# Two transformer blocks on one core: ten of twelve modulation parts summed on VectorE from transposed weight tiles, gates by way of DRAM, weights and vectors packed by the host

## The chip, the cores and the metric

The kernel runs on one core of a Trainium2 chip. The metric is the device time of one execution in microseconds (us), lower is better. Everything is float32 in and out.

## What is computed

Two transformer blocks are applied to 256 latent tokens of width 1024, beside 256 context tokens. Block 1 has two layers, whose normed inputs are scaled and shifted, and whose outputs are gated, by a *modulation* of a conditioning vector:

```
mod  = silu(c)     @ ada_w[l] + ada_b[l]         # latent: six vectors of 1024 per layer
modc = silu(c_ctx) @ ada_w[l][:, :n] + ada_b[l]  # context: six in layer 0, two in layer 1
a    = rms_norm(h, g) * (1 + sc1) + sh1;  h = h + g1 * mixer(a)
a    = rms_norm(h, g) * (1 + sc2) + sh2;  h = h + g2 * ffn(a)
```

Layer 0 mixes by a gated convolution and a neighbourhood attention (8 heads, latent and context tokens) and has a dense FFN (hidden width 2816). Layer 1 mixes by a windowed attention (8 heads) and a differential attention (4 heads), for the latent tokens alone, and has a mixture of 8 experts, two per token. Block 2 (a dilated and a latent attention, an MLP of 4096) has no modulation. The modulation is 12 *parts* of 1024 columns of `ada_w`, 4 MB each: 48 MB of weights for a product with one or two vectors.

## The kernel before

**Products.** Every float32 matmul is three products of rounded parts: ACT writes `hi`, a rounded copy of a weight tile (line 1184), VectorE writes `lo`, the rest (line 1704), and TensorE makes low by high, high by low and high by high (`mm3`, lines 722 to 724).

**Weight tiles.** All weights pass as tiles of up to 128 x 2048 floats (1 MB) in one list, in the order in which TensorE uses them, through *slots* of SBUF: three that are always there, four more in the start, one more (`slot_f`) in the FFN. The SP queue issues the loads in list order; each waits until the slot's tile before has been consumed (lines 2669, 2670). ACT and VectorE run their programs strictly in order. Before they wait for a product of TensorE, they call `feed(event)`, which makes the hi or lo of every tile that stands less than `ahead` places behind the tiles used at that event (`next_tiles`, line 486). `ahead` is 4 in the start and 2 after it.

**Modulation.** `MODS` (line 409) lists the 12 parts. Each half of 512 columns takes two tiles. `mod_product` (lines 767 to 781) makes 8 matmuls of 4 x 512 outputs per tile; VectorE copies the row out of PSUM (line 1762); POOL loads the bias beside it by a DMA (line 2553); `mod_spread` turns the row into a column per vector (line 797) or, for the gates (parts 2, 5, 10, 11), spreads it over 128 partitions (line 791); VectorE (line 1772) or ACT (line 1226 on) copies that out. Parts 0 and 1 (shift and scale of layer 0) come first of all. The rest are *filler*, written by a generator that yields between other steps: parts 2, 3, 4 in the steps of layer 0's attention `a0`, five fillings per part spread over its first 15 of 39 steps; parts 5 to 9 in the FFN, a tile after each of the w1 and w3 tiles; parts 10 and 11 in the first 10 steps of layer 1's attention `a1`. The line numbers of the generators: 800 (TensorE), 1238 (ACT), 1775 (VectorE), 2555 (POOL).

**Order of work.** Start (parts 0 and 1, norm) to 64 us; layer 0 projections (75 to 205: q, v, k, then the convolution's c, u, g twice, 12 tiles; VectorE norms the heads of q and k, lines 1794 to 1798, with a power on POOL, line 2569, in the middle, and scales and splits the turned heads, lines 1989 and 1709); POOL adds masks to the position biases (line 2600); `a0` (210 to 358); output product and norm; FFN (434 to 850); norm; layer 1 projections (884 to 985, 9 tiles, `odd_unit`, line 2125); `a1` from 1000; mixture of experts (1247 to 1572, with its tail to 1640); block 2 to the end. In an attention VectorE takes the row maxima of a unit (head and token tile, line 1903), ACT the exponentials, TensorE the transposes and the product with v, three (`a0`) or two (`a1`) steps later.

**Start.** ACT's queue issues the constants, some 18 small vectors (line 1316) and the four token tiles; TensorE turns the vectors into columns `VT`; ACT takes their silu (line 1322).

```
        def next_tiles(at, *events):
            ...
            if t.gate != at["gate"] or t.slot not in at["slots"] or i >= n + at["ahead"] or (t.prev is not None and t.prev > n - 2):
                return
```

## Time and profile before

| | |
|---|---|
| median of three runs | 2158.98 us (2157.37 to 2165.85) |
| the profiled execution's own time | 2171.43 us |
| its span on the core | 2169.6 us |
| granted TensorE clock, mean | 0.89 of full speed |
| busy: PE / VectorE / ACT / POOL | 88% / 56% / 41% / 6% |
| read from HBM | 325.8 MB, mean 151 GB/s |

Times in a row are microseconds from the start of the span unless ns is said. PE is TensorE's matmuls, PEld its weight loads, DVE is VectorE, SP the queue that loads the weights. The clock is a share of 2.4 GHz: 1.00 or 0.50 (1.2 GHz) at any moment, a mean in between over a stretch.

### The profile page before, as it was taken

What the parts mean: (1) busy time and instruction counts of PE and PEld (TensorE: products, weight loads), DVE (VectorE), ACT (ScalarE), POOL (GpSimd) and SP (SyncE); (2) the same over time, 40 slices, a digit from 0 to 9 for tenths busy, and PEclk for the clock granted to TensorE, in tenths of its full rate; (3) what the DMA queues carried; (4) which work ended last, traced back from release to release, by engine and by line L of the source; (5) the groups of instructions that cost most, each with busy time, mean ns of one, the idle gap of its engine ahead of it and who ended that gap; (6) DMA issues with size and microseconds to landing.
All of it is one profiled execution on the core that took longest, in us unless ns stands there. A gap on an engine that the chain in (4) does not pass through costs nothing. (4 is left out here: it accounts for less than half of the span.)

```text
span 2169.6 us, 22152 instructions
## 1 busy us (share of the span) xinstructions
PE 1915.4 (88%) x9060; PEld 1545.3 (71%) x9060; DVE 1206.3 (56%) x1520; ACT 898.3 (41%) x1044; POOL 125.7 (6%) x128
## 2 busy tenths in 40 slices
PE   5899899699999997795876999999995999796997
PEld 2777468577787775582655888888885966676986
DVE  5465443344433442545563888888885545456643
ACT  5323432343313331423332676767763442334542
POOL 1130000200020002112001000000000000000000
PEclk9999776889999998796677899999998995797999
DMA  6433330234434442223204699999973640125653
GB/s 243 117 97 117 98 97 12 86 117 136 150 107 140 137 150 79 83 78 97 78 1 140 221 328 329 324 325 325 326 263 128 197 141 0 59 78 165 185 188 113
DMA packets 190860, 328.44 MB, mean 151 GB/s; under 512 B 17358, under 2 KB 90512, under 8 KB 190751
## 3 DMA queue, kind: packets, MB, share of 16 engines
q1 hardware_dynamic: 185712, 321.54, 44.0%
q10 hardware_dynamic: 4208, 5.27, 0.8%
q8 instruction: 75, 1.23, 0.2%
q0 software_dynamic: 832, 0.13, 0.0%
q14 instruction: 33, 0.27, 0.0%
HBM read 325.81 MB, written 1.11 MB: 151 GB/s over the span
## 5 line engine op out<-in xcount | busy, mean ns | idle before, releaser
L1704 DVE TENSOR_TENSOR wlo__60<-raw__59,whi__61 128x2048 fp32r<-128x2048 f32 (+3 forms) x73 | 163.1, 2235 | 136.9 <-ACT whi__61 L1184 136.8
L1704 DVE TENSOR_TENSOR wlo__63<-raw__62,whi__64 128x2048 fp32r<-128x2048 f32 (+3 forms) x73 | 151.2, 2072 | 122.7 <-ACT whi__64 L1184 122.7
L1704 DVE TENSOR_TENSOR wlo__66<-raw__65,whi__67 128x2048 fp32r<-128x2048 f32 (+3 forms) x72 | 156.1, 2168 | 105.0 <-ACT whi__67 L1184 104.9
L1184 ACT ACTIVATE whi__61<-raw__59 128x2048 fp32r<-128x2048 f32 (+3 forms) x73 | 133.1, 1824 | 125.8 <-DMA raw__59<-in_ffn_w 39.3
L1184 ACT ACTIVATE whi__64<-raw__62 128x2048 fp32r<-128x2048 f32 (+3 forms) x73 | 123.7, 1694 | 137.3 <-DMA raw__62<-in_ada_w 38.2
L1184 ACT ACTIVATE whi__67<-raw__65 128x2048 fp32r<-128x2048 f32 (+3 forms) x72 | 130.7, 1815 | 97.0 <-DMA raw__65<-in_ada_w 25.4
L2569 POOL TENSOR_TENSOR keep__55<-keep__55,keep__56 128x1 f32<-128x1 f32 (+3 forms) x48 | 45.4, 946 | 1219.9 <-DVE keep__55 L1714 1219.9
L1903 DVE TENSOR_REDUCE keep__55<-ps 128x1 f32<-128x256 f32 (+1 forms) x104 | 56.6, 544 | 46.4 <-PE ps L724 39.6
L1704 DVE TENSOR_TENSOR wlo__210<-raw__209,whi__211 128x2048 fp32r<-128x2048 f32 x24 | 54.8, 2285 | 4.0 <-ACT whi__211 L1184 4.0
L1704 DVE TENSOR_TENSOR wlo__213<-raw__212,whi__214 128x2048 fp32r<-128x2048 f32 x24 | 54.8, 2284 | 0.0
L1704 DVE TENSOR_TENSOR wlo__216<-raw__215,whi__217 128x2048 fp32r<-128x2048 f32 (+1 forms) x24 | 50.6, 2109 | 3.8 <-ACT whi__217 L1184 3.8
L1704 DVE TENSOR_TENSOR wlo__133<-raw__132,whi__134 128x2048 fp32r<-128x2048 f32 (+2 forms) x14 | 28.9, 2064 | 40.5 <-ACT whi__134 L1184 40.5
L722 PE MATMUL ps<-ffn__113,wlo__133 128*128 128x512 f32 x112 | 45.1, 403 | 7.0 <-DVE wlo__133 L1704 7.0
L1184 ACT ACTIVATE whi__211<-raw__209 128x2048 fp32r<-128x2048 f32 x24 | 45.8, 1907 | 7.1 <-DMA raw__209<-in_moe_w 7.1
L1184 ACT ACTIVATE whi__214<-raw__212 128x2048 fp32r<-128x2048 f32 x24 | 45.9, 1911 | 6.3 <-DMA raw__212<-in_moe_w 6.1
L723 PE MATMUL ps<-ffn__114,whi__134 128*128 128x512 f32 x112 | 44.6, 399 | 0.0
L724 PE MATMUL ps<-ffn__113,whi__134 128*128 128x512 f32 x112 | 44.6, 398 | 0.0
L1184 ACT ACTIVATE whi__217<-raw__215 128x2048 fp32r<-128x2048 f32 (+1 forms) x24 | 42.6, 1773 | 3.4 <-DMA raw__215<-in_moe_w 2.9
L1184 ACT ACTIVATE whi__134<-raw__132 128x2048 fp32r<-128x2048 f32 (+2 forms) x14 | 24.2, 1727 | 44.5 <-DMA raw__132<-in_ffn_w 34.5
L722 PE MATMUL ps<-ffn__113,wlo__66 128*128 128x512 f32 x96 | 37.6, 392 | 0.0
L724 PE MATMUL ps<-ffn__113,whi__67 128*128 128x512 f32 x96 | 37.4, 390 | 0.0
L723 PE MATMUL ps<-ffn__114,whi__67 128*128 128x512 f32 x96 | 37.4, 389 | 0.0
(1082 smaller groups left out, 5645.4 us busy)
## 6 DMA issues: line engine op xcount, KB each, us to landing
raw__209<-in_moe_w SPq DMA_DIRECT2D x24, 1024.0 KB, 6.4
raw__212<-in_moe_w SPq DMA_DIRECT2D x24, 1024.0 KB, 6.9
raw__215<-in_moe_w SPq DMA_DIRECT2D x16, 1024.0 KB, 5.9
raw__65<-in_moe_w SPq DMA_DIRECT2D x16, 1024.0 KB, 6.2
raw__59<-in_moe_w SPq DMA_DIRECT2D x16, 1024.0 KB, 7.1
raw__65<-in_ada_w SPq DMA_DIRECT2D x14, 1024.0 KB, 5.2
raw__59<-in_ada_w SPq DMA_DIRECT2D x13, 1024.0 KB, 5.2
raw__62<-in_ada_w SPq DMA_DIRECT2D x13, 1024.0 KB, 5.2
```

Of the source, the lines that this page charges most:

```text
L722: e.matmul(out, ll, rh, start=start, stop=False)
L723: e.matmul(out, lh, rl, start=False, stop=False)
L724: return e.matmul(out, lh, rh, start=False, stop=stop)
L1184: e.activation(t.hi(), t.raw(), ACT.Copy).then_inc(*did("hi", i))
L1704: e.tensor_tensor(t.lo(), t.raw(), t.hi().bitcast(F32), ALU.subtract).then_inc(*did("lo", i))
L1903: e.tensor_reduce(neg, b[:, 0:u.total], AX.X, ALU.max).then_inc(*link())
L2569: e.tensor_tensor(x, x, EXPO[:, 0:1].broadcast_to([128, n_]) if n_ > 1 else EXPO[:, 0:1], ALU.pow).then_inc(*did(out, *key))
```

## The change

- **Sums.** Parts 2 to 11 are no longer products. The host transposes their columns of `ada_w`; a tile holds two blocks of 128 columns, a column per partition and its 1024 weights along the partition. VectorE multiplies a block with the row silu(c) or silu(c_ctx), which lies in all 128 partitions (`CB`), and adds up in the same instruction: two (parts 8 to 11) or four (parts 2 to 7) instructions of 1024 elements per tile, each waiting for the one before; then a small addition of the bias per part. ACT skips these tiles and TensorE has nothing to do with them, except for the gates.
- **Places.** A sum tile stands in the list behind each weight tile, one by one: 12 (parts 2, 3, 4) from the first tile of layer 0's projections, 20 (5 to 9) from the first of the FFN (into the w2 tiles), 8 (10, 11) from the first of layer 1's projections. `next_tiles` counts them as tiles, with `ahead` as before. The filler in `a0`, FFN and `a1` is gone.
- **Gates.** The sums of a gate are turned by TensorE, copied by VectorE, written to DRAM by POOL's queue and read back as a row into 128 partitions by a second DMA that waits for the first: parts 2 ahead of `a0`, 5 behind the first half of w1 and w3, 10 and 11 one behind the other ahead of `a1`.
- **Start.** One DMA brings all vectors, already turned. Two DMAs of 512 KB bring the broadcast rows c and c_ctx on ACT's queue behind the token tiles; ACT waits for them and takes silu of 128 x 2048 before its first `hi`. The start has five more slots, not four.
- **Packing.** Every weight tile lies in DRAM as 128 rows of up to 8 KB, one per partition; before a row was 1, 1.5, 2 or 4 KB of the weight matrix.
- Some buffers are placed anew; ACT no longer waits for the bias scratch (`rp2`), POOL does.

The core of the diff:

```diff
+    def of(self, arrays):
+        x = arrays[self.name][tuple(slice(*p) if isinstance(p, tuple) else p for p in self.at)]
+        x = x.T if self.turned else x
+        k, n = x.shape[0] // 128, x.shape[1]
+        return x.reshape(k, 128, n).transpose(1, 0, 2).reshape(-1)
...
-    slot_e = [slot(WORK + n) for n in (0, 4096)] + [slot(WORK + n) for n in (10240, 14336)]
+    slot_e = [slot(WORK + n) for n in (0, 4096, 14336, 18432, 22528)]
```

TensorE: a sum tile behind each consumed tile, and the gates.

```diff
+        def sums(p, jj):
+
+            l, part = MODS[p][:2]
+            o = part * D + jj * 256
+            i = state["tile"]
+            state["tile"] += 1
+            if book.counting:
+                src = W["ada_w"][l, :, o:o + 256].t()
+                packed.place(src)
+                s = min(open_slots, key=lambda s: last_in.get(s, s - 100))
+                TILES.append(Tile(src, 2, 1024, s, last_in.get(s), ""))
+                TILES[i].sums, TILES[i].done = (p, jj), ("msum", p, jj)
+                last_in[s] = i
+
+        def gate_rows(p):
+            n = 8 * MODS[p][3]
+            b = take("6", "gt", p)
+            for s, n_ in state["due"](("gsum", p)):
+                e.wait_ge(s, n_)
+            tr(b[0:n, 0:128], GM_OF[p][:, 0:n]).then_inc(*done("gt", p))
+
         def consumed(t, *event):
             t.done = event
+            for p, jj in itertools.islice(state["sums"], 1):
+                sums(p, jj)
 
...
         rdy = lambda N: (lambda t, k: normed(N, t // 2))
-        w_ev = I["ev_w_in"][0]
+        w_ev = W["ev_w_in"][0]
+        state["sums"] = iter([(p, jj) for p in (2, 3, 4) for jj in range(4)])
         proj(("l0", "q"), x4(AT4a), 4, KT, w_ev[:, 1536:2048], 512, rdy("a"))
...
-        fill = modulation([5, 6, 7, 8, 9], "7")
+        state["sums"] = iter([(p, jj) for p in (5, 6, 7, 8, 9) for jj in range(4)])
         nf = normed("f", 0) + normed("f", 1)
         for blk in range(2):
             bs = slice(blk * 1408, (blk + 1) * 1408)
             for f0 in range(0, 11, 2):
                 m = min(2, 11 - f0)
-                feat(("ff1", blk, f0), AT4f, I["ffn_w1"][0][:, bs], f0, m, 512, nf, "7")
```

ACT: the start, and the tiles that it passes over.

```diff
+                if t.sums:
+                    continue
                 for s, n in due((f"raw{t.slot}", i)):
                     e.wait_ge(s, n)
                 e.activation(t.hi(), t.raw(), ACT.Copy).then_inc(*did("hi", i))
...
-        for s, n in due(("z_vr",)):
-            e.wait_ge(s, n)
-        for i, (o, src) in enumerate(vec_loads):
-            e.dma_start(o, src).then_inc(*did("vec", *([i] if i + 1 < len(vec_loads) else []), by=16))
+        e.dma_start(VT[:, 0:sum(n for _, n in VECTORS)], I["vectors"]).then_inc(*did("vt", by=16))
         for t in range(4):
             e.dma_start(h_t[t], xs_d[t]).then_inc(*did("d_x", *([t] if t < 3 else []), by=16))
-        feed(("vt_t",))
+        for v, x in enumerate((I["c"], I["c_ctx"].rearrange("(o n) -> o n", o=1))):
+            e.dma_start(CB[:, v * D:(v + 1) * D], x.broadcast_to([128, D])).then_inc(
+                *did("d_cb", *([] if v else [v]), by=16))
         for s, n in due(("vt",)):
             e.wait_ge(s, n)
         e.activation(SM[:, 24:40], VT[:, 0:16], ACT.Silu).then_inc(*did("silu"))
         high("stq_hi", (), STQ[:, :, 0:2], SM[:, 24:40].rearrange("p (v k) -> p k v", v=2), ("silu",))
+        for s, n in due(("d_cb",)):
+            e.wait_ge(s, n)
+        e.activation(CB, CB, ACT.Silu).then_inc(*did("cb"))
```

VectorE: the sums and the gates' copy.

```diff
+                    summed(i, t)
+                    continue
                 for s, n in due(("hi", i)):
                     e.wait_ge(s, n)
                 e.tensor_tensor(t.lo(), t.raw(), t.hi().bitcast(F32), ALU.subtract).then_inc(*did("lo", i))
+
+        def summed(i, t):
+            p, jj = t.sums
+            gate, nv = MODS[p][3], vectors_of(p)
+            for s, n in due((f"raw{t.slot}", i), ("cb",), *gm_free(p)):
+                e.wait_ge(s, n)
+            for c in range(2):
+                for v in range(nv):
+                    k = 2 * jj + c
+                    x = GM_OF[p][:, v * 8 + k:v * 8 + k + 1] if gate else MODT_OF[p][:, 2 * k + v:2 * k + v + 1]
+                    junk = slot_sum[t.slot][:, (c * nv + v) % 2 * 1024:(c * nv + v) % 2 * 1024 + 1024]
+                    m = e.scalar_tensor_tensor(out=junk, in0=slot_raw[t.slot][:, c * 1024:c * 1024 + 1024], scalar=1.0,
+                                               in1=CB[:, v * D:(v + 1) * D], op0=ALU.mult, op1=ALU.mult, accum_out=x)
+                    if (c, v) == (1, nv - 1):
+                        m.then_inc(*did("msum", p, jj))
+                    elif v == nv - 1:
+                        m.then_inc(*link())
+                        for s, n in linked():
+                            e.wait_ge(s, n)
+            if jj < 3:
+                return
+            l, part = MODS[p][:2]
+            bias = VT[:, VROW["ada_b"] + l * 48 + part * 8:VROW["ada_b"] + l * 48 + part * 8 + 8]
+            for s, n in due(("msum", p, 3)):
+                e.wait_ge(s, n)
+            if gate:
+                x, b3 = v3(GM_OF[p][:, 0:8 * nv], nv), bias.rearrange("p (o k) -> p o k", o=1).broadcast_to([128, nv, 8])
+            else:
+                x = MODT_OF[p].rearrange("p (k v) -> p k v", v=2)[:, :, 0:nv]
+                b3 = bias.rearrange("p (k o) -> p k o", o=1).broadcast_to([128, 8, nv])
+            e.tensor_tensor(x, x, b3, ALU.add).then_inc(*did("gsum" if gate else "spr", p))
+
+        def gate_rows(p):
+            n_ = 8 * MODS[p][3]
+            feed(("gt", p))
+            for s, n in due(("gt", p), *([("gw", past_gate(p))] if past_gate(p) else [])):
+                e.wait_ge(s, n)
+            e.tensor_copy(G16[0:n_, :], bank("gt", p)[0:n_, 0:128]).then_inc(*did("gcp", p))
+            empties(("gt", p), ("gcp", p))
 
         def low(name, key, dst, src, hi, *events):
```

POOL: the gates by way of DRAM. SP: the packed loads.

```diff
+        def gate_rows(p):
+            n_ = MODS[p][3]
+            rows = scr_d["gates"][p, 0:n_ * D]
+            for s, n in due(("gcp", p)):
+                e.wait_ge(s, n)
+            e.dma_start(rows.rearrange("(r c) -> r c", c=128), G16[0:8 * n_, :]).then_inc(*did("gw", p, by=16))
+            for s, n in due(("gw", p), *row_free(p)):
+                e.wait_ge(s, n)
+            e.dma_start(MODS[p][2], rows.rearrange("(o n) -> o n", o=1).broadcast_to([128, n_ * D])).then_inc(
+                *did("sprb", p, by=16))
...
+                w_ = t.k * t.n
+                src = bass.AP(tensor=I[t.src.name].tensor, offset=packed.place(t.src), ap=[[w_, 128], [1, w_]])
+                e.dma_start(slot_raw[t.slot][:, 0:w_], src).then_inc(*did(f"raw{t.slot}", i, by=16))
```

## Rows read from the trace of the kernel before

**Rows 1.** Page: busy time of each engine; chain that ended last, by engine
```profile
PE 1915.4 (88%) x9060; PEld 1545.3 (71%) x9060; DVE 1206.3 (56%) x1520; ACT 898.3 (41%) x1044; POOL 125.7 (6%) x128
...
PE 19%; DVE 2%; ACT 1%; issue 1%; DMA 1%; POOL 0%; ACTq 0%; POOLq 0%; DVEq 0%
```

**Rows 2.** Stretches of time: length, busy us of each engine, clock, DMA
```profile
75.00:205.00 130.00, 126.40 (x567) 104.27 (x566) 70.34 (x73) 36.97 (x37) 25.41 (x12) 0.99 0.31 99
...
312.00:362.00 50.00, 48.49 (x200) 42.12 (x200) 17.21 (x49) 14.06 (x45) 0.00 (x0) 0.50 0.00 1
...
488.00:814.00 326.00, 325.73 (x1447) 252.64 (x1446) 136.73 (x110) 103.03 (x86) 17.12 (x15) 1.00 0.42 137
...
1062.00:1100.00 38.00, 38.00 (x160) 32.24 (x159) 19.05 (x46) 12.28 (x30) 0.00 (x0) 0.50 0.00 0
...
1247.00:1572.00 325.00, 322.13 (x1618) 273.81 (x1617) 285.60 (x221) 228.64 (x201) 0.00 (x0) 1.00 0.93 326
```

**Rows 3.** Stretch 434 to 868, three answers: PE's lines 778, 797, 791 alone
```profile
434.00:868.00 434.00, 40.35 (x160) 13.54 (x160) 0.97 0.39 127
...
434.00:868.00 434.00, 8.39 (x64) 7.70 (x64) 0.97 0.39 127
...
434.00:868.00 434.00, 3.96 (x8) 1.32 (x8) 0.97 0.39 127
```

**Rows 4.** Durations (ns, min/median/max) of two VectorE forms: lines 2355 and 2030
```profile
L2355 DVE TENSOR_TENSOR moe__188<-moe__188,keep__54 x1: 1225/1225/1225, 1636.6 to 1636.6; 128x1024 f32<-128x1024 f32 x1
...
L2030 DVE SCALAR_TENSOR_TENSOR in__82<-in__85,keep__51,in__82 x1: 753/753/753, 172.0 to 172.0; 128x512 f32<-128x512 f32 x1
```

**Rows 5.** Start: median landing of the last ACT loads, then ACT's first and eighth hi
```profile
keep__50<-in_ctx ACTq DMA_DIRECT2D x2, 512.0 KB, 10.6
...
10.90 1.91 ACT L1184 ACTIVATE whi__61<-raw__59 128x2048 fp32r<-128x2048 f32 x1
...
31.48 1.92 ACT L1184 ACTIVATE whi__61<-raw__59 128x2048 fp32r<-128x2048 f32 x1 [0.67 <-DMA raw__59<-in_ada_w]
```

**Rows 6.** Timeline of VectorE, layer 0 projections: start, duration, what it waited for
```profile
86.56 2.29 DVE L1704 TENSOR_TENSOR wlo__63<-raw__62,whi__64 128x2048 fp32r<-128x2048 f32 x1 [1.62 <-ACT whi__64 L1184]
...
101.16 0.69 DVE L1798 TENSOR_TENSOR in__80<-ps,keep__55 128x512 f32<-128x512 f32 x1 [1.75 <-POOL keep__55 L2569]
...
143.00 6.12 DVE L1704 TENSOR_TENSOR wlo__60<-raw__59,whi__61 128x2048 fp32r<-128x2048 f32 x1
```

**Rows 7.** Timeline of POOL, layer 0 projections
```profile
142.32 4.65 POOL L2600 TENSOR_TENSOR in__75<-in__75,keep__49 128x2048 f32<-128x2048 f32 x1
```

**Rows 8.** Timeline of VectorE, first attention: row maxima, one per unit
```profile
209.82 0.69 DVE L1903 TENSOR_REDUCE keep__55<-ps 128x1 f32<-128x512 f32 x1
...
312.78 0.42 DVE L1903 TENSOR_REDUCE keep__55<-ps 128x1 f32<-128x256 f32 x1 [1.81 <-PE ps L724]
...
316.36 0.42 DVE L1903 TENSOR_REDUCE keep__55<-ps 128x1 f32<-128x256 f32 x1 [2.97 <-PE ps L724]
...
339.02 0.42 DVE L1903 TENSOR_REDUCE keep__55<-ps 128x1 f32<-128x256 f32 x1 [1.69 <-PE ps L724]
...
341.32 0.42 DVE L1903 TENSOR_REDUCE keep__55<-ps 128x1 f32<-128x256 f32 x1 [1.26 <-PE ps L724]
```

**Rows 9.** Timeline of VectorE, layer 1 projections: first evacuation
```profile
901.84 0.68 DVE L1794 TENSOR_REDUCE keep__55<-odd__171 128x8 f32<-128x512 f32 x1
...
913.33 0.69 DVE L2143 TENSOR_TENSOR odd__166<-odd__166,odd__170 128x512 f32<-128x512 f32 x1 [1.37 <-POOL odd__170 L2632]
```

**Rows 10.** Timeline of VectorE, window attention: row maxima, one per unit
```profile
1002.48 0.69 DVE L1903 TENSOR_REDUCE keep__55<-ps 128x1 f32<-128x512 f32 x1
...
1061.36 0.69 DVE L1903 TENSOR_REDUCE keep__55<-ps 128x1 f32<-128x512 f32 x1
...
1087.16 0.69 DVE L1903 TENSOR_REDUCE keep__55<-ps 128x1 f32<-128x512 f32 x1
```

**Rows 11.** DMA issues in 985 to 1065: bias load by POOL, KB, us to landing
```profile
keep__57<-in_ada_b POOLq DMA_DIRECT2D x2, 2.0 KB, 2.7
```

More of the change, by code:

```diff
@@ L486, in next_tiles @@
     def next_tiles(at, *events):
-        n = max(place[event] for event in events)
+        n = max([place[event] for event in events], default=0)
         while at["tile"] < len(TILES):
@@ L681, in tensor_program @@
         due = Due(book)
-        state = dict(tile=0, due=due, gate="")
+        state = dict(tile=0, due=due, gate="", sums=iter(()))
         open_slots, turn_of = [0, 1, 2] + slot_e, Counter()
@@ L827, in attend @@
             A = HEADS[st]
-            fill = modulation(A.fill, "5")
-            per = -(-5 * len(A.fill) // len(A.units))
             for i in A.steps():
@@ L878, in attend @@
                     m.then_inc(*done("fin", st, g))
-                for _ in range(per):
-                    next(fill, None)
-            for _ in fill:
-                pass
         def head_turn(key, src, n, ready, ring="8"):
@@ L1258, in attend @@
             A = HEADS[st]
-            fill = modulation(A.fill)
-            per = -(-5 * len(A.fill) // len(A.units))
             for i in A.steps():
@@ L1403, in scalar_program @@
                     feed(("prod", "ff2", blk, half, t))
-        for _ in fill:
-            pass
         over = [("prod", "ff2", 1, 1, 3)]
@@ L1884, in attend @@
             A = HEADS[st]
-            fill = modulation(A.fill)
-            per = -(-5 * len(A.fill) // len(A.units))
             for i in A.steps():
@@ L1945, in attend @@
                     empties(("fin", st, g), ("flo", st, g))
-                for _ in range(per):
-                    next(fill, None)
-            for _ in fill:
-                pass
         def gated(stage, half, t, bk, g, tmp, *events):
@@ L2601, in gpsimd_program @@
                             ALU.add).then_inc(*did("bm", t))
-        for _ in modulation(HEADS["a0"].fill):
-            pass
+        gate_rows(2)
         for half in range(2):
@@ L2608, in gpsimd_program @@
             norm_rsqrt("f", t)
-        fill = modulation([5, 6, 7, 8, 9])
         for blk in range(2):
-            for _ in range(12):
-                next(fill, None)
+            if blk == 0:
+                gate_rows(5)
             for half in range(2):
@@ L2615, in gpsimd_program @@
                     residual(("ff2", blk), half, t, TMPf[t])
-        for _ in fill:
-            pass
         for t in range(4):
@@ L2633, in gpsimd_program @@
                 m.then_inc(*did("orp", kind, t))
-        for _ in modulation(HEADS["a1"].fill):
-            pass
+        gate_rows(10)
+        gate_rows(11)
         for g in (2, 3):
```

325 lines of the change are left out of this document (150 added, 175 removed).

## The prediction

> **What bounds the kernel now.** I read the page first. TensorE is busy 88% of the span, and in the chain that ended last it has 19%, DMA 1% [rows 1]. So the end is TensorE's program plus the stretches in which TensorE waits for somebody. Then I read the stages, since the share is an average of unlike ones [rows 2]. In the FFN (488 to 814) TensorE is busy all of 326 us at full clock, and VectorE 42% of it: what is taken from TensorE there comes off the time. In the expert stage TensorE has 322 of 325 us while DMA is at 0.93 of its share: TensorE bounds, narrowly. In the layer 0 projections it has 126 of 130 us, at 0.99. In the tail of `a0` (312 to 362), without filler, TensorE looks busy (48 of 50 us) but at 0.50, which is 1.2 GHz, with small matmuls; the same in `a1` behind its filler (1062 to 1100). There the steps set the pace, and the clock sets the steps.
>
> **The price of the modulation on TensorE.** In 434 to 868 its products have 160 matmuls and 40.4 us, the spreads 8.4 and 4.0 us [rows 3]. Overlap of neighbours makes the first too large: 1447 matmuls in 325.7 us [rows 2] are 0.225 each, so 160 are 36 us. Together 48 us.
>
> **The price on VectorE.** No row shows a multiplication with a sum taken along. The nearest: two inputs in SBUF, 1024 elements, 1.22 us; a scalar_tensor_tensor of 512 elements, 0.75 [rows 4]. The slope of the first (about 0.53 per 512) on top of the second gives 1.28, which I take, since it is the same operation; the ends are 1.22 and, if the read-out of the sum costs as much again as half an instruction, 1.9. So 5.1 us per tile for two vectors, 2.6 for one: 24 x 5.1 + 16 x 2.6 = 164 us of VectorE, for 40 lo of 2.3 (92) removed. On the whole span that is little; where it falls decides.
>
> A rule speaks against it. The Trainium skill, "Vector Engine (DVE) Microarchitecture Reference", section "Points that are easy to get wrong", says that a scalar_tensor_tensor with two sources in SBUF that aren't bf16 runs at half throughput, as both read ports are taken and none is left for the accumulator. The row of 0.75 us has two such sources but reads out no sum, so it can't settle it. By the rule a sum would be about 2.5 us; the sum below goes by 1.28, and the rule is the fourth rival.
>
> **Part by part.**
>
> *Start.* The last token tiles land 10.6 us after their issue, beside SP's tiles; ACT's first hi is at 10.90, its eighth at 31.48 [rows 5]. Now ACT waits, ahead of every hi, for two more DMAs of 512 KB on the same queue. The 2 MB of tokens took these 11 us, so 1 MB more takes some 5.5; the issue comes about 6 us earlier, for 17 small DMAs are gone: landing at about 20 to 21, silu of 128 x 2048 as long as a hi (1.9): first hi at 23. Queued behind it are all hi, so all lo. Eight lo of 2.3 end at 23 + 1.9 + 18.3 = 43.2; before, 31.48 + 1.92 + 2.3 = 35.7. That is +7.5. `ahead` of 4 puts the first sum tile (5.1) in front of the third row copy: together **+13**. Ends: +2 (rows early, sum in a gap) and +23 (rows land only with SP's eighth tile, at about 31).
>
> *Layer 0 projections.* 12 tiles in 130 us, 10.8 each [rows 2]. The lookahead of two tiles is now a weight tile and a sum, so one weight tile. VectorE makes v's second lo at 86.56 and then norms q's heads until 101.85 [rows 6]: 13.0 us, in which TensorE had v's two tiles. Now the first sum (5.1) stands ahead of v's first lo, and v's second lo comes after the norms, another sum and itself: 13.0 + 5.1 + 2.3 = 20.4 against 10.8 of cover, a stall of 9.6. With the first 5.1 it is 14.7, and the same behind k's heads: 29.4. The four groups behind (c with the turned k, u, g, u again) I put at 3 each; POOL's two mask additions (4.65 the first [rows 7]) made a lo 6.12 instead of 2.29 [rows 6], and now a sum can be the one that is stretched. Together **+41**. Ends: +2 (VectorE's 70.3 + 12 x 5.1 = 131.5 us against the stage's 130) and +61 (all twelve sums on the path).
>
> *`a0`.* The first 16 units take 209.82 to 312.78, 103 us, with all filler [rows 8]. Without it I expect the slow clock of the tail [rows 2]. There a light step takes 2.30 (339.02 to 341.32), a light one whose earlier heavy units are finished beside it 3.58 (312.78 to 316.36) [rows 8]: a heavy second half costs 1.28 more, and a heavy first half about as much: 4.9. 13 x 4.9 and three opening steps of 2.4 are 71: **-32**. Ends: -24 and -67 (everything at 2.4 GHz, half of 71).
>
> *FFN.* -48 on TensorE. VectorE goes from 137 us of 326 [rows 2] to about 172 of 278, so sums fit, but one may stand ahead of a needed lo, and POOL's residuals stretch some: +4. **-44**; ends -53 (rows 3 as they stand) and -30.
>
> *Layer 1 projections.* A pair of units takes VectorE 901.84 to 914.0, 12.2 us [rows 9], and again only one weight tile is ahead; a sum is 2.6 here. The second dq tile waits 12.2 + 2.6 + 2.3 less a cover of 5.4 (two token tiles instead of four, half of 10.8): 11.7. The second dv tile: 17.1 less 10.8, 6.3. The second dk tile behind the small units about the same, 6.3. With one sum and its wait at the front (4): **+28**; ends 0 and +35.
>
> *`a1`.* Nine steps take 1002.48 to 1061.36, 58.9 us, with filler; behind it six take 1061.36 to 1087.16, 4.30 each at 0.50 [rows 10, 2]. Nine of these are 38.7: **-20**; ends -15 and -39.
>
> *Gates.* Those of parts 2 and 5 are covered by units and w2 tiles, which reach their first gate tens of us later. Part 11's copy waits until part 10's rows are in DRAM, with nothing on VectorE ahead of the first maximum of `a1`: a small DMA by POOL lands in 2.7 us [rows 11], with the issue **+4**; ends 0 and +8.
>
> *Packing.* The expert stage has 3 us without TensorE in 325 [rows 2]; elsewhere tiles land ahead. **-3**; ends 0 and -22 (all of DMA's 1% in the chain [rows 1]). The bytes stay the same.
>
> Sum: +13 +41 -32 -44 +28 +4 -20 -3 = -13, against the profiled execution's 2171.4. That execution stands 0.6% above the median of the runs, 2159.0; so I predict 2159.0 - 13 = **2146**. A measurement tells about 0.5% (11 us) from no change.
>
> **The rivals.**
>
> 1. *The clock stays up.* If without filler `a0` and `a1` run at 2.4 GHz, they give 35 and 19 us more: 2092; as VectorE's and ACT's steps don't halve, rather 2105. For it: with filler the stretches held the clock partly. Against: the two stretches without filler are at 0.50 throughout [rows 2].
>
> 2. *The projections lose more than the attentions gain* (the other side). Its place is VectorE's queue in the two projection stages: a sum ahead of each needed lo, with one tile of lookahead. Start +23, layer 0 +61, layer 1 +35, gates +8, FFN -34, the rest as above: -34 -32 -20 -3 + 127 = +38, 2197. It decides once these costs pass the 99 us that `a0`, FFN, `a1` and packing give; my own terms stand at 86.
>
> 3. *The packed rows bring more*: all of DMA's share of the chain, -22 instead of -3, and 15 of the stalls above: 2112 to 2127. Against: TensorE is busy 322 of 325 us where DMA is fullest [rows 2].
>
> 4. *A sum costs double.* Tiles take 10 and 5 us. VectorE then needs 70 + 120 us in layer 0's projections, over the 171 that I give them: +50; layer 1 +15, FFN (172 + 80 of 278) +8: +60 in all, 2219. This is the skill's rule.
>
> **How the numbers follow.** Forecast 0.41, centre -13, some 15 either way: faster 0.22, same 0.16, slower 0.03. Rival 1 0.22, faster. Rival 2 0.22: slower 0.17, same 0.05. Rival 3 0.07, faster. Rival 4 0.06, slower. The rest 0.02, slower. Faster 0.51, same 0.21, slower 0.28. The forecast's own range is 2125 to 2170. The range for 8 in 10 is 2098 to 2198: it leaves out the lower third of rival 1, the top of rival 2 and rival 4.
>
> **What would show it.** First hi near 23. A sum of 1.28 us in the rows of VectorE (2.5: rival 4). TensorE idle some 10 us inside v and c, waiting for a lo whose VectorE row follows head norms and a sum. The first maximum of `a0` about 54 later than before, and a row to the tail of `a0` of about 71 us for 16 units, at 0.50. FFN without lines 778 to 797, still full, some 44 shorter. The first maximum of `a1` reached behind a wait for a DRAM write. I am wrong if the projections stay at 10.8 a tile, if the clock is near 1.00 in `a0`, or if the expert stage shrinks.

## The result and the profile after

The changed kernel takes 2189.5 us (median of four runs, 2189.4 to 2192.8), the kernel before 2162.2 in the same runs: a ratio of **1.013**, 95% interval 1.010 to 1.016. It is slower by 1.3%, where I had forecast 0.6% faster. The time lies inside the range (2098 to 2198), near the value of rival 2 (2197), the one on the other side.

The page of the changed kernel, busy time and the chain that ended last:

```profile
PE 1852.4 (85%) x8622; PEld 1542.0 (70%) x8622; DVE 1259.7 (57%) x1716; ACT 818.5 (37%) x992; POOL 119.5 (5%) x116
...
PE 19%; DVE 2%; ACT 1%; issue 1%; DMA 1%; POOL 0%; ACTq 0%; POOLq 0%; DVEq 0%
```

TensorE has 63 us less to do than in [rows 1], and the span is 21 us longer. VectorE has 53 us more. The chain names the same owners as before, so it does not say where the time went; the stages do. Windows of the changed kernel (length, then busy us of PE, PEld, DVE, ACT, POOL, then clock, DMA share, GB/s): layer 0 projections, heavy half of `a0`, FFN, layer 1 projections, `a1`'s first ten units, expert stage.

```profile
85.00:288.00 203.00, 156.63 (x641) 124.85 (x641) 128.43 (x174) 40.09 (x41) 23.13 (x10) 0.86 0.38 132
...
288.00:360.00 72.00, 70.23 (x249) 55.11 (x250) 19.51 (x43) 15.98 (x39) 1.14 (x2) 0.50 0.04 15
...
484.00:862.00 378.00, 367.38 (x1585) 301.70 (x1585) 197.24 (x232) 87.40 (x80) 22.13 (x15) 0.98 0.40 145
...
892.00:1042.00 150.00, 99.85 (x444) 80.47 (x444) 82.78 (x174) 33.92 (x42) 29.44 (x29) 0.81 0.32 119
...
1042.00:1073.00 31.00, 28.59 (x121) 26.02 (x122) 14.81 (x34) 8.47 (x21) 1.61 (x3) 0.50 0.11 34
...
1229.00:1655.00 426.00, 421.12 (x2070) 356.55 (x2070) 368.08 (x279) 298.39 (x259) 0.00 (x0) 1.00 0.84 311
```

The same stages of the kernel before (`a1`'s are in [rows 10], the expert stage in [rows 2]):

```profile
62.00:210.00 148.00, 144.40 (x634) 117.12 (x634) 75.69 (x81) 38.33 (x41) 25.41 (x12) 0.97 0.34 103
...
210.00:313.00 103.00, 89.08 (x397) 53.74 (x395) 50.47 (x65) 41.24 (x56) 1.94 (x4) 0.79 0.37 122
...
437.00:852.00 415.00, 414.73 (x1815) 321.98 (x1815) 167.52 (x130) 128.01 (x105) 24.20 (x20) 0.99 0.40 130
...
884.00:1002.00 118.00, 92.92 (x431) 76.13 (x432) 62.26 (x140) 31.23 (x39) 29.89 (x30) 0.85 0.25 81
```

Between fixed events of the two profiled executions the account is this. The events are the first product of a stage, the first row maximum of an attention, and, where the FFN and the rest of `a1` end, TensorE's first turn for the next norm; so the row of the layer 1 projections includes that norm:

| stretch | before | after | difference | predicted |
|---|---|---|---|---|
| start, to the first layer 0 product | 61.6 | 85.2 | +23.6 | +13 |
| layer 0 projections, to the first maximum of `a0` | 148.2 | 202.7 | +54.6 | +41 |
| `a0`, the 16 heavy units | 103.0 | 72.7 | -30.2 | -32 |
| rest of `a0`, output product, norm | 124.2 | 123.3 | -0.9 | 0 |
| FFN | 429.3 | 390.8 | -38.5 | -44 |
| layer 1 projections with the two gates | 136.2 | 167.7 | +31.5 | +32 |
| `a1`, ten units | 58.9 | 30.4 | -28.5 | -20 |
| rest of `a1`, output product | 110.8 | 113.6 | +2.8 | 0 |
| router, to the first expert product | 32.6 | 42.3 | +9.7 | 0 |
| expert stage, block 2 | 964.8 | 962.1 | -2.6 | -3 |

The sum of the differences is +21.4 (2191.0 against 2169.6). The medians stand further apart, 27 us, because the profiled execution of before is 9 us above its median and that of the changed kernel 3 us above its own. The kernel before spreads widely: over the 31 runs that stood beside the first experiments it went from 2144.9 to 2175.5 with a median of 2158.1, while the changed kernel's four lie within 3.5 us.

**Start.** ACT's timeline, then TensorE's first layer 0 product:

```profile
32.46 1.91 ACT L1366 ACTIVATE silu_rows<-silu_rows 128x2048 f32<-128x2048 f32 x1 [22.08 <-DMA silu_rows<-in_c_ctx]
...
34.28 1.89 ACT L1257 ACTIVATE whi__62<-raw__60 128x2048 fp32r<-128x2048 f32 x1
...
47.92 1.90 ACT L1257 ACTIVATE whi__108<-raw__106 128x2048 fp32r<-128x2048 f32 x1
```

```profile
85.21 0.77 PE L822 MATMUL ps<-whi__62,in__85 128*128 128x512 f32 x1 [4.88 <-ACT in__87 L1292]
```

ACT sat 22.1 us for the broadcast row of c_ctx, and all eight hi are behind it: the first at 34.28 instead of 10.90 [rows 5]. The two issues that ended last (KB, us to landing) left at 4.67 and 4.79 us and landed together at 32.3 and 32.4:

```profile
raw__106<-in_ada_w SPq DMA_DIRECT2D x1, 1024.0 KB, 27.6
...
silu_rows<-in_c_ctx ACTq DMA_DIRECT2D x1, 512.0 KB, 27.6
```

That is the condition of my term's upper end: the rows landed only with SP's eighth tile.

**Layer 0 projections.** VectorE makes a lo, norms q's heads, does the waiting sum and then the lo that TensorE needs; below it TensorE's wait for that lo, and the load of a weight tile that SP can issue only when the sum has freed its slot:

```profile
109.34 2.29 DVE L1744 TENSOR_TENSOR wlo__65<-raw__64,whi__66 128x2048 fp32r<-128x2048 f32 x1 [0.87 <-ACT whi__66 L1257]
...
123.95 0.69 DVE L1860 TENSOR_TENSOR xs__79<-ps,keep__58 128x512 f32<-128x512 f32 x1 [1.75 <-POOL keep__58 L2620]
...
124.56 1.21 DVE L1756 SCALAR_TENSOR_TENSOR wsum__71<-raw__68,silu_rows 128x1024 f32<-128x1024 f32 x1
...
129.25 0.08 DVE L1756 DVE_READ_ACCUMULATOR wsum__71<-raw__68,silu_rows 128x1 f32 x1
```

```profile
131.68 0.76 PE L822 MATMUL ps<-whi__62,in__85 128*128 128x512 f32 x1 [8.74 <-DVE wlo__61 L1744]
```

```profile
129.36 0.33 SPq L2721 DMA_DIRECT2D raw__68<-in_ev_w_in  x1
```

TensorE waited 8.7 us for the lo of v's second tile, where I had worked out 9.6. What I had not counted stands in the windows: TensorE is *busy* 156.6 us here instead of 144.4, for the same matmuls, because the clock is 0.86 instead of 0.97. Ahead of the wait above it, behind it and a few us later:

```profile
118.00:122.00 4.00, 4.00 (x19) 3.31 (x18) 2.21 (x5) 0.75 (x1) 1.64 (x1) 1.00 0.00 0
...
133.00:137.00 4.00, 4.00 (x11) 3.03 (x11) 3.93 (x8) 1.91 (x1) 0.00 (x0) 0.50 0.11 45
...
140.00:143.00 3.00, 3.00 (x15) 2.45 (x15) 0.27 (x1) 0.60 (x1) 0.00 (x0) 1.00 0.00 0
```

It is at 2.4 GHz until the wait, at 1.2 for the 5 us behind it, and then up again. So some 42 us of the 54.6 are waits and 12 are slower matmuls. And the load at 129.36 comes right after the sum's last instruction: a slot that holds a sum stays taken until VectorE's turn, and landing (4.7 us) and hi follow only then.

The two longest waits of the stage have something else in them. In the first, the two sums that run beside POOL's mask additions take 5.0 and 5.5 us instead of 1.22, and the lo that TensorE waits for stands behind them:

```profile
191.48 5.50 DVE L1756 SCALAR_TENSOR_TENSOR wsum__67<-raw__64,silu_rows 128x1024 f32<-128x1024 f32 x1
...
190.44 5.47 POOL L2653 TENSOR_TENSOR in__83<-in__83,keep__49 128x2048 f32<-128x2048 f32 x1
...
201.71 0.77 PE L822 MATMUL ps<-in__84,wlo__69 128*128 128x512 f32 x1 [10.69 <-issue]
```

In the second, VectorE itself is idle for 10.8 us, waiting for the *load* of a sum tile (issued at 214.66), while the step that TensorE waits for (VectorE takes k's turned heads out of PSUM and scales them) stands behind that sum in its order:

```profile
219.53 1.23 DVE L1756 SCALAR_TENSOR_TENSOR wsum__71<-raw__68,silu_rows 128x1024 f32<-128x1024 f32 x1 [10.80 <-DMA raw__68<-in_ada_w]
...
225.04 1.12 PE L828 MATMUL ps<-keep__49,xs__79 128*128 128x128 f32 x4 [9.53 <-DVE xs__78 L2040]
```

So a sum costs here by its time on VectorE and also by the place it takes in the lists.

**The sum itself** (line 1756; ns, min/median/max, in the FFN) costs what a plain product costs:

```profile
L1756 DVE SCALAR_TENSOR_TENSOR wsum__67<-raw__64,silu_rows x32: 1212/1220/2198, 483.8 to 686.1; 128x1024 f32<-128x1024 f32 x32
...
L1756 DVE DVE_READ_ACCUMULATOR wsum__67<-raw__64,silu_rows x32: 74/81/84, 485.0 to 688.2; 128x1 f32 x32
```

1.22 us and 0.08 for reading out the sum, 4.9 us per tile for two vectors, wherever POOL leaves it alone.

**FFN.** TensorE is busy 367.4 us of 378 instead of 414.7 of 415: the 47.3 us that leave it are the 48 of [rows 3]. But it now has holes of 10.6 us. The two largest are where the first half of w1 and w3 ends: the first ends with the last lo, which VectorE makes behind a sum (until 603.60), the second with the copy of the gate, also behind a sum (until 615.79):

```profile
603.70 0.47 PE L822 MATMUL ps<-ffn__124,wlo__69 128*128 128x512 f32 x1 [2.67 <-issue]
...
615.90 0.76 PE L822 MATMUL ps<-whi__145,ffn__132 128*128 128x512 f32 x1 [4.76 <-issue]
```

**The gates of `a1`.** POOL's two issues for part 10, the write and the read back:

```profile
1039.14 0.62 POOL L2610 DMA_DIRECT2D gate_scratch<-keep__55  x1 [4.52 <-DVE keep__55 L1782]
...
1042.05 0.56 POOL L2613 DMA_DIRECT2D keep__57<-gate_scratch  x1 [2.29 <-DMA gate_scratch<-keep__55]
```

The write has landed 2.3 us after its issue was done, and VectorE stands idle for it:

```profile
1041.85 0.28 DVE L1782 COPY keep__55<-ps 8x128 f32<-8x128 f32 x1 [3.01 <-DMA gate_scratch<-keep__55]
```

Its first maximum of `a1` is at 1042.5, behind this copy.

**The router.** The load of 32 KB (KB, us to landing) and TensorE's wait for it. Nothing in the change touches it:

```profile
moe__193<-in_moe_router ACTq DMA_DIRECT2D x1, 32.0 KB, 18.8
```

```profile
1202.17 4.19 PE L1057 MATMUL ps<-moe__193,moe__204 128*128 128x8 f32 x19 [8.37 <-DMA moe__193<-in_moe_router]
```

It lands 18.8 us after its issue; before, it was 10.9. TensorE waits 8.4 us for it.

### The profile page after: what moved, and what is told of

Same layout as the page of the kernel before. It is cut to its first block and busy times, and to the rows that moved or that the text cites. A ratio compares the mean times of both kernels' runs of the same rounds, so it can differ in the third digit from the quotient of the medians.

```text
span 2191.0 us, 21341 instructions
## 1 busy us (share of the span) xinstructions
PE 1852.4 (85%) x8622; PEld 1542.0 (70%) x8622; DVE 1259.7 (57%) x1716; ACT 818.5 (37%) x992; POOL 119.5 (5%) x116
## 5 line engine op out<-in xcount | busy, mean ns | idle before, releaser
L1744 DVE TENSOR_TENSOR wlo__69<-raw__68,whi__70 128x2048 fp32r<-128x2048 f32 (+3 forms) x65 | 142.5, 2193 | 65.3 <-ACT whi__70 L1257 65.2
L1744 DVE TENSOR_TENSOR wlo__61<-raw__60,whi__62 128x2048 fp32r<-128x2048 f32 (+4 forms) x57 | 111.4, 1954 | 94.7 <-ACT whi__62 L1257 94.6
L1257 ACT ACTIVATE whi__70<-raw__68 128x2048 fp32r<-128x2048 f32 (+3 forms) x65 | 118.3, 1820 | 113.4 <-DMA raw__68<-in_ffn_w 55.2
L1744 DVE TENSOR_TENSOR wlo__65<-raw__64,whi__66 128x2048 fp32r<-128x2048 f32 (+3 forms) x55 | 116.0, 2110 | 45.6 <-ACT whi__66 L1257 45.5
L1257 ACT ACTIVATE whi__66<-raw__64 128x2048 fp32r<-128x2048 f32 (+3 forms) x55 | 97.4, 1770 | 111.1 <-DMA raw__64<-in_ev_w_in 44.2
L1257 ACT ACTIVATE whi__62<-raw__60 128x2048 fp32r<-128x2048 f32 (+4 forms) x57 | 93.6, 1642 | 99.2 <-DMA raw__60<-in_ev_w_out 27.8
L1756 DVE SCALAR_TENSOR_TENSOR wsum__67<-raw__64,silu_rows 128x1024 f32<-128x1024 f32 x54 | 74.3, 1403 | 11.4 <-DMA raw__64<-in_ada_w 10.8
L1756 DVE SCALAR_TENSOR_TENSOR wsum__63<-raw__60,silu_rows 128x1024 f32<-128x1024 f32 x52 | 63.8, 1255 | 28.4 <-DMA raw__60<-in_ada_w 27.9
L822 PE MATMUL ps<-ffn__124,wlo__144 128*128 128x512 f32 x144 | 57.3, 398 | 8.2 <-DVE wlo__144 L1744 7.0
L823 PE MATMUL ps<-ffn__125,whi__145 128*128 128x512 f32 x144 | 56.9, 395 | 0.0
L824 PE MATMUL ps<-ffn__124,whi__145 128*128 128x512 f32 x144 | 56.7, 394 | 0.0
L822 PE MATMUL ps<-ffn__124,wlo__69 128*128 128x512 f32 x136 | 53.6, 394 | 2.7 <-issue 2.7
L824 PE MATMUL ps<-ffn__124,whi__70 128*128 128x512 f32 x136 | 53.6, 394 | 0.0
L823 PE MATMUL ps<-ffn__125,whi__70 128*128 128x512 f32 x136 | 53.5, 393 | 0.0
L1257 ACT ACTIVATE whi__223<-raw__221 128x2048 fp32r<-128x2048 f32 x24 | 45.9, 1911 | 7.0 <-DMA raw__221<-in_moe_w 7.0
```

The source lines that it names most:

```text
L822: e.matmul(out, ll, rh, start=start, stop=False)
L823: e.matmul(out, lh, rl, start=False, stop=False)
L824: return e.matmul(out, lh, rh, start=False, stop=stop)
L1257: e.activation(t.hi(), t.raw(), ACT.Copy).then_inc(*did("hi", i))
L1744: e.tensor_tensor(t.lo(), t.raw(), t.hi().bitcast(F32), ALU.subtract).then_inc(*did("lo", i))
L1756: m = e.scalar_tensor_tensor(out=junk, in0=slot_raw[t.slot][:, c * 1024:c * 1024 + 1024], scalar=1.0, in1=CB[:, v * D:(v + 1) * D], op0=AL ...
```

## The experiments

All were run beside the kernel before, so I compare ratios to it (the changed kernel: 1.013) and, within profiles, the same stretches.

**Old rows.** The changed kernel loads its ordinary tiles in rows of the weight matrix again; only the sums' tiles are packed.

```diff
+                if t.sums:
                     src = bass.AP(tensor=I["turned"].tensor, offset=packed.place(t.src), ap=[[w_, 128], [1, w_]])
...
+                else:
+                    src = I[t.src.name][tuple(slice(*p) if isinstance(p, tuple) else p for p in t.src.at)]
+                    e.dma_start(t.raw(), src.rearrange("(k p) n -> p k n", p=128)).then_inc(
```

> The changed kernel with the old rows: all weight tiles as in the kernel before (rows of 1 to 4 KB per partition), only the turned tiles of the sums stay packed in 8 KB rows. Theory A (the DMA engines take packets of the two queues in turn, so 8 KB packets on SP's queue hold back the small packets of ACT's queue): the silu rows land at about 24 us instead of 32.5, the first layer 0 matmul starts near 77 instead of 85.2; the router's 32 KB land about 11 us after issue instead of 18.8, and the 8.4 us that TensorE waits for them vanish. Together 15 to 18 us less than the changed kernel, less about 3 that the packed rows gave in the expert stage: about 2175. Theory B (the packing has no part in it, the rows land late because of the bytes ahead of them): landings as in the changed kernel, 2190 to 2193.

Measured: 2171.6 us, ratio 1.004 (1.001 to 1.007). The silu of the rows in ACT's timeline, and the router's landing:

```profile
19.24 1.91 ACT L1365 ACTIVATE silu_rows<-silu_rows 128x2048 f32<-128x2048 f32 x1 [11.62 <-DMA silu_rows<-in_c_ctx]
```

```profile
moe__193<-in_moe_router ACTq DMA_DIRECT2D x1, 32.0 KB, 11.0
```

ACT got the rows 13.2 us earlier, the first layer 0 product came at 72.0 instead of 85.2, both 5 us better than I had set, and the router landed as before the change. Theory A holds on both counts, and theory B, by which the landings would not have moved, falls. The packing, which I had put down as a gain of 3 us, costs this kernel some 18. And the gain itself doesn't show: from the first expert product to the end the old rows take 961.7 us, the packed ones 962.1.

**Packing alone**, on the kernel before (the same two lines of the load and of the host's layout).

> The kernel before with packed weight rows and nothing else. Theory A: the router lands about 19 us after its issue instead of 10.9 and the expert stage starts 8 us later; the token tiles land a few us later in the start, where ACT needs them only at 27.9, so little there; some 3 us are won in the expert stage and behind: 3 to 7 us slower than before. Theory B: router as before, 0 to 5 us faster.

Measured: 2167.3 us, ratio 1.003 (0.999 to 1.007). By time alone this decides nothing, since the interval holds 1. By the profile it does: from the turn for the router's product to the first expert product it is 41.7 us against 32.6, and the router:

```profile
moe__181<-in_moe_router ACTq DMA_DIRECT2D x1, 32.0 KB, 18.2
```

In the start nothing moved (first layer 0 product 61.7), as ACT has nothing to wait for there. The profile also shows where the spread of the kernel before may come from. The light half of `a0` in this execution:

```profile
309.00:340.00 31.00, 30.24 (x169) 25.54 (x167) 14.89 (x45) 12.19 (x40) 0.00 (x0) 0.75 0.00 1
```

The clock was 0.75 there (1.00 from 309 to 320, 0.50 from 330 on), and the 16 light units went from 308.8 to 339.5, 31 us, where the kernel before has 41 at 0.50, from 312.8 to 353.7 [rows 2, 8]. The instructions of that stretch are the same in both; the clock is sometimes up and sometimes down.

**Router in 128 packets.** The host lays the router out as one row of 256 bytes per partition.

```diff
-        e.dma_start(RW, I["moe_router"][0].rearrange("(k p) e -> p k e", p=128)).then_inc(*did("rw", by=16))
+        e.dma_start(RW, I["moe_router"].rearrange("p (k e) -> p k e", k=KT)).then_inc(*did("rw", by=16))
```

> The changed kernel with the router's 32 KB laid out by the host as one row of 256 bytes per partition (128 packets instead of 1024). Theory A: with an eighth of the packets to take turns for, it lands within 7 us of its issue, the wait of 8.4 us on TensorE vanishes, 8 to 10 us faster than the changed kernel: about 2180. Theory B (bytes ahead of it): lands at 17 to 19 as now, no change.

Measured: 2183.6 us, ratio 1.011 (1.008 to 1.014). That is 5.8 us under the changed kernel's median, less than the 8 to 10 that I had set; the two intervals overlap. In the profiles the router's stretch is 34.0 us instead of 42.3.

```profile
moe__193<-in_moe_router ACTq DMA_DIRECT2D x1, 32.0 KB, 8.2
```

It lands in 8.2 us, a little more than I had set, but ahead of the turns, and the 8.4 us of wait are gone. The bytes ahead of it were the same: it was the way its 32 KB were cut, 1024 packets of 32 bytes or 128 of 256, that made it late.

**Silu rows late.** ACT waits for the broadcast rows behind the second half part's hi, not ahead of the first.

```diff
-        for s, n in due(("d_cb",)):
-            e.wait_ge(s, n)
-        e.activation(CB, CB, ACT.Silu).then_inc(*did("cb"))
         at["ahead"] = 4
         for g in range(4):
             feed(("mod", g // 2, g % 2, 1))
+            if g == 1:
+                for s, n in due(("d_cb",)):
+                    e.wait_ge(s, n)
+                e.activation(CB, CB, ACT.Silu).then_inc(*did("cb"))
```

> The changed kernel, but ACT waits for the silu rows and computes them behind the hi of the second half part instead of ahead of the first. If the wait ahead of all hi is what costs the start: first hi at about 11, landing-bound hi until about 32, first layer 0 matmul at 64 to 70 instead of 85.2, the whole time 15 to 20 us less than the changed kernel (about 2171). If the start is bound by the landing of the tiles and the extra sum instead: 3 to 6 us less.

Measured: 2171.0 us, ratio 1.007 (1.003 to 1.010). ACT's first hi and the silu:

```profile
10.26 1.89 ACT L1257 ACTIVATE whi__62<-raw__60 128x2048 fp32r<-128x2048 f32 x1
...
34.13 1.90 ACT L1370 ACTIVATE silu_rows<-silu_rows 128x2048 f32<-128x2048 f32 x1
```

The first layer 0 product came at 65.7 instead of 85.2, the projections behind it took 202.4 us as in the changed kernel. The wait ahead of all hi was most of the cost of the start (19.5 of 23.6 us), and it carried through to the end (18.5 us by the medians).

**Sums cut short.** Only 32 of 1024 elements of the sums of parts 2 to 4.

```diff
+                    w_ = 32 if p < 5 else 1024
-                    m = e.scalar_tensor_tensor(out=junk, in0=slot_raw[t.slot][:, c * 1024:c * 1024 + 1024], scalar=1.0,
+                    m = e.scalar_tensor_tensor(out=junk[:, 0:w_], in0=slot_raw[t.slot][:, c * 1024:c * 1024 + w_], scalar=1.0,
```

> The changed kernel with the sums of parts 2, 3 and 4 cut to 32 of 1024 elements; their tiles are still loaded and still stand in the list (the output lacks most of these parts). It parts VectorE's time from the lost lookahead in the layer 0 projections, which take 202.7 us there (85.2 to 287.9) against 148.2 before. If the sums' own time is the cost (12 x 4.9 = 59 us on VectorE), the stage falls to about 150 to 155. If the single tile of lookahead is (v's second lo behind 13 us of head norms), it stays at 175 or more.

Measured: one run, 2169.4 us; the projections from 81.2 to 266.6, 185.3 us. The window of the stage:

```profile
81.00:266.00 185.00, 156.79 (x641) 125.20 (x641) 83.10 (x172) 39.96 (x41) 22.16 (x10) 0.90 0.40 145
```

VectorE has 45 us less to do than in the changed kernel, and the stage gets only 17 shorter. 37 of the 54.6 us stay with the sums all but gone: about 25 are waits, and the 12 of slower matmuls have not gone at all (TensorE is busy 156.8 us as in the changed kernel). They come with the places that the sum tiles take, as the next run shows. That was the side of the theory of the single tile of lookahead; how the 25 us divide between that tile, the slots that are freed only in VectorE's order and VectorE's waits for the sum tiles' loads, no run tells.

**Sums in `a0`.** A sum tile behind each of the first 12 units' scores, and the gate at step 12 (SP's first batch of loads grows by a tile, so that the start has what it feeds).

```diff
-        def attend(st):
-            A = HEADS[st]
+        def attend(st, fill=(), gates={}):
+            A, fill = HEADS[st], iter(fill)
             for i in A.steps():
+                if i in gates:
+                    gate_rows(gates[i])
...
+                for p, jj in itertools.islice(fill, 1):
+                    sums(p, jj)
...
-        state["sums"] = iter([(p, jj) for p in (2, 3, 4) for jj in range(4)])
-        gate_rows(2)
-        attend("a0")
+        attend("a0", [(p, jj) for p in (2, 3, 4) for jj in range(4)], {12: 2})
```

> The changed kernel with the 12 sum tiles of parts 2, 3, 4 placed in the first 12 steps of a0, not between the tiles of the layer 0 projections; the gate of part 2 is turned at step 12. If lookahead and sums in the projections are what costs them, the stage goes from 202.7 us to about 148 (-54). In a0 VectorE has 0.26 of 69 us busy, so 59 us of sums nearly fill it: a0's first 16 units go from 72.7 to 80 to 90 (+8 to +17). Whole: 35 to 45 us less than the changed kernel, about 2150. If the rival holds (the projections are slow for another reason, such as the late start and POOL's additions), the stage stays above 180.

Measured: 2151.2 us, ratio 0.997 (0.994 to 1.000). Projections and heavy half of `a0`:

```profile
83.00:229.00 146.00, 142.68 (x637) 116.66 (x636) 77.71 (x93) 32.34 (x36) 24.31 (x10) 0.98 0.31 101
...
229.00:320.00 91.00, 73.27 (x257) 55.67 (x255) 70.59 (x129) 20.87 (x42) 1.14 (x2) 0.51 0.42 143
```

The stage is back at 146.7 us, at a clock of 0.98. In `a0` VectorE rises from 19.5 to 70.6 us busy, and the heavy units take 91.0 us instead of 72.7: +18.3, a little over what I had set. The trade wins 38 us, in the account of the stages and in the medians.

**Sums in `a1` too**, parts 10 and 11 in its first eight steps, gates at steps 8 and 12.

> As e6_moved0, and the 8 sums of parts 10 and 11 in the first 8 steps of a1, with their gates at steps 8 and 12. Layer 1 projections: from 149.9 us (892.6 to 1042.5) to about 118 as before; a1's first ten units from 30.4 to 32 to 38. Another 22 to 30 us less than e6_moved0: about 2125.

Measured: 2129.6 us, ratio 0.986 (0.981 to 0.991), 22 us less than the one before. The layer 1 projections from their first product to the first maximum went from 149.9 to 116.6 us, against the 118 that I had set, the stretch of `a1`'s ten units from 30.4 to 39.5, a little more than the 32 to 38. The whole is at the lower edge of the 22 to 30 that I had set.

**All of it**: sums in both attentions, silu rows late, router in 128 packets.

> Everything that the runs so far favour: e7_moved with the silu rows behind the second pair of products (e4_late, 20 us) and the router in 128 packets (e3_router, 8 to 9 us). If the parts add up: 26 to 29 us below e7_moved, about 2098, which is 2.8% below the kernel before. If the start and the projections share one wait, less than 20 below e7_moved.

Measured: **2101.9 us, ratio 0.974** (0.969 to 0.978). The parts add up, 27.7 us below the kernel without the last two. Its windows of the layer 0 projections, of `a0`'s heavy half and of `a1`'s first ten units:

```profile
63.00:210.00 147.00, 143.55 (x637) 117.60 (x637) 77.85 (x94) 32.83 (x37) 24.29 (x10) 0.97 0.32 99
...
211.00:302.00 91.00, 72.41 (x255) 55.20 (x256) 70.24 (x130) 20.37 (x42) 1.14 (x2) 0.52 0.41 141
...
982.00:1022.00 40.00, 39.51 (x168) 35.21 (x169) 19.99 (x42) 12.04 (x26) 2.24 (x4) 0.50 0.08 28
```

It beats both kernels: 2.6% under the one before, and it is the changed kernel's idea with the sums elsewhere.

**Half rows and quarter rows.** The packed layout, cut so that no packet is over 4 KB, or over 2 KB.

```diff
-        return x.reshape(k, 128, n).transpose(1, 0, 2).reshape(-1)
+        return x.reshape(k, 128, n).transpose(1, 0, 2).reshape(128, 2, k * n // 2).transpose(1, 0, 2).reshape(-1)
...
+                src = bass.AP(tensor=I[t.src.name].tensor, offset=packed.place(t.src),
+                              ap=[[q_, 128], [128 * q_, 2], [1, q_]])
```

> The changed kernel with every packed tile stored and loaded as two half rows per partition (packets of at most 4 KB, not 8), same bytes, same order. Theory A (turns by packet): the router lands between the 11.0 us of 2 KB packets and the 18.8 us of 8 KB: 12 to 15; the silu rows, themselves packets of 4 KB, between the 19.2 and 32.5 us at which ACT got them: 22 to 27. If it is the contiguous layout in DRAM and not the packet that matters, both stay at 18.8 and 32.5.

Measured: one run, 2180.6 us. Silu rows and router:

```profile
23.52 1.91 ACT L1366 ACTIVATE silu_rows<-silu_rows 128x2048 f32<-128x2048 f32 x1 [15.39 <-DMA silu_rows<-in_c_ctx]
```

```profile
moe__193<-in_moe_router ACTq DMA_DIRECT2D x1, 32.0 KB, 16.4
```

> As e9_half with quarter rows (packets of at most 2 KB) out of the packed layout. Theory A: as with the old rows: router 11 us after issue, silu rows at ACT by 19 to 21, first layer 0 matmul near 72, though the weights lie packed. If the layout matters: as the changed kernel.

Measured: one run, 2180.7 us.

```profile
19.29 1.91 ACT L1366 ACTIVATE silu_rows<-silu_rows 128x2048 f32<-128x2048 f32 x1 [11.63 <-DMA silu_rows<-in_c_ctx]
```

```profile
moe__193<-in_moe_router ACTq DMA_DIRECT2D x1, 32.0 KB, 11.0
```

With packets of SP's queue of 8, 4 and 2 KB, ACT gets the rows at 32.5, 23.5 and 19.3 us, and the router lands in 18.8, 16.4 and 11.0 us (16.4 is above the 12 to 15 that I had set). The landings in the start show the turns themselves. ACT's loads there have 128 packets of 4 KB each. With 8 KB on SP's queue, 128 packets per tile, one tile and one load of ACT land side by side every 3.8 us. With 4 KB, 256 packets per tile, a load of ACT lands every 2.6 us and a tile every 5.0: packet for packet again. With 2 KB it is 2.0 and 5.4 us, about three packets of SP to two of ACT. It is the packet, not the layout in DRAM: quarter rows out of the packed layout behave as the old rows. The time of the quarter rows is 9 us above that of the old rows all the same, most of it behind the start: 4 us in layer 0's projections and 4 in the FFN. One run each; that difference stays open.

**The best kernel with old rows.**

> e8_best with the old weight rows (and so without need of the packed router, which is as before). Tells what the packing is worth once its harm is taken away: the expert stage is bound by TensorE, so within 5 us of e8_best, more likely 0 to 4 us slower (2102 to 2106). If packed rows speed the stages that wait for tiles (norm to first product, the last projections), 8 us slower or more.

Measured: 2108.2 us (2106.2 to 2111.7), ratio 0.977 (0.972 to 0.982). That is 6 us more than with packed rows, over the 0 to 4 that I held likeliest; the two stood beside different runs of the kernel before, and the intervals of their ratios overlap. In the profiles (one each) the start is 2.6 us longer, the FFN 3.1 and the router, whose 1024 packets are back, 0.8, while the expert stage and block 2 are 1.9 us shorter. Once nobody waits for small packets, packing is worth a few us at most.

## Why the prediction was wrong

Three places carry the miss: the start (+10.6 over its term), layer 0's projections (+13.6) and the router (+9.7, no term at all). They make up 33.9 of the 34.4 us by which the account of the stages (+21.4) stands above mine (-13); the other steps are off too and cancel. By its own steps, in their order:

- *Start, +13.* **This term failed**: +23.6. I had the wait and what was queued behind it, but I let the rows land after 20 us by dividing bytes by a rate, as if the packing had no part. The runs show that SP's packet size sets the landing: with old rows ACT had the silu rows at 19.2, with packed ones at 32.5. That is the direction in which it goes when the two queues' packets are taken in turn. With old rows the start is +10.4 (72.0 against 61.6), near my 13; the 13.2 us of later landing are what the term lacked. So the term came out at its upper end, +23, whose condition (rows land only with SP's eighth tile) is what happened.
- *Layer 0 projections, +41.* **This term was mis-sized**: +54.6. The mechanism was right, to a stall (8.7 us where 9.6 was worked out). The waits together came to some 42 against my 41, though not one by one as I had them: the first sum cost 2.6 us and not 5.1, the sums beside POOL's additions more. What was left out is the clock, 12 us of slower matmuls after the waits. That the places cost more than the sums' time was shown by cutting the sums: 37 us remain.
- *`a0`, -32* and *`a1`, -20.* `a0` gave 30.2. Its clock is 0.50 from end to end, as forecast; a heavy unit takes 5.67 us, not 4.9, but the opening steps are nearly free. `a1` gave 28.5: its opening steps too take 1.3 us and not 4.2, since their scores are ready behind the gates' wait.
- *FFN, -44.* -38.5. The saving on TensorE was 47.3 of 48; the holes cost 10.6 and not 4.
- *Layer 1 projections and gates, +28 and +4.* +31.5, in part by luck: all of my 32 were waits, while in the windows 25 us are idle time of TensorE and 7 are slower matmuls, which no term of mine had.
- *Packing, -3.* **This term failed**, and in sign: +9.7 at the router, which no step of mine named, and some 13 in the start. The -2.6 in the expert stage and behind looks like my -3 and isn't shown to be the packing's: the changed kernel with old rows takes 961.7 us there, not more. The kernel before with packed rows took 960.8 instead of 964.8, one profile each. I had looked at what packing does to its own transfers, and not at whom they share the engines with.
- *The base.* I worked from a profiled execution 9 us above the kernel's median, so the differences between profiles (+21.4) come out 6 us smaller than between medians (+27). That the light half of `a0` is that spread is suggested by one other profile (0.75 there) and not shown.

Rival 2 named the side, the place and the point: costs above 99 us turn the sign. They came to 23.6 + 54.6 + 31.5 + 9.7 + 2.8 = 122, against 101 of gains. Its layer 0 term (+61) was nearer than mine; without the packing's 18 to 23 us the changed kernel stands at the kernel before or 0.4% above (old rows: 1.004). So my account of the sums, by itself, would still have been too favourable by some 20 us. That the time lies inside the range is no merit of the forecast, which was 43 us too low.

Rival 4, the rule of the Trainium skill ("Vector Engine (DVE) Microarchitecture Reference", "Points that are easy to get wrong") that two float32 sources halve the throughput, does not hold here: 1.22 us with the sum taken along, as a plain product of the same size takes [rows 4]. Beside POOL's additions it took 5.0 and 5.5, which is another matter: a lo is stretched there too [rows 6]. (The +50 that I gave rival 4 in layer 0 doesn't follow from its own numbers: 190 us of VectorE over 171 are 19.) Rival 1 fell: the clock was 0.50 in both attentions. Rival 3 fell too: of the stages behind the start, none is longer with old rows than with packed ones by more than 1.4 us.

For the turns between queues the Trainium skill has the sentence that I should have weighed: "DMA: Bandwidth & Descriptors", section "Queues, rings and completion order", says that each engine takes the queues in turn, a packet at a time. By it a queue's share grows with its packets, and the 32.5, 23.5 and 19.3 us above agree. The page's packet is a bundle of descriptors and need not be the profile's; that a row of 8 or 4 KB takes a turn of its own is read from the landings above, and with 2 KB they fit less well.

## What to carry to other kernels

Work that leaves the busiest engine still needs a place in the order of the engine that takes it: put between products that wait for the same engine it costs more than it saves (+54.6 for 12 sums between projections), put where that engine idles it pays (the same sums in the attention: the time 38 us lower). When transfers are made larger, look for small transfers of another queue that run at the same time and that somebody waits for; count their packets. And take the difference from a median, or from several profiles, when the kernel's own spread is as large as the forecast.

## What the runs showed of the hardware

- The landing of a transfer on one queue depends on the packet size of the other queue: the same 32 KB in 1024 packets took 11.0, 16.4 and 18.8 us beside packets of 2, 4 and 8 KB, and 8.2 us beside 8 KB when it was 128 packets. 1 MB in 128 packets of 8 KB and 512 KB in 128 packets of 4 KB, on two queues, land together, pair by pair, every 3.8 us.
- Multiplication with a running sum over 1024 float32 elements takes VectorE 1.22 us, the read-out 0.08; beside POOL's additions of 128x2048 (4.6 and 5.5 us) two such sums took 5.0 and 5.5.
- TensorE's clock was 0.50 through all of `a0` without modulation matmuls (busy 111.2 of 113 us by the profile, 288 to 401), and its mean was 0.50 and 0.75 in the same light stretch of two executions with equal instructions there; in the layer 0 projections the waits brought its mean from 0.97 to 0.86 and made the same matmuls 12 us longer.
